# Gathering expert rows of U and V together, 8 KB each, into five joint buffers

## What is computed

```python
def block(xt):                                   # 128 tokens at a time
    qry = (xt @ w_query).reshape(128, 8, 2, 128)
    s1 = einsum('thd,kd->thk', qry[:, :, 0], keys1)
    s2 = einsum('thd,kd->thk', qry[:, :, 1], keys2)
    # top 16 of each, top 16 of their 256 sums: idx, gate
    act = gelu(einsum('td,thkd->thk', xt, expert_u[idx]))
    return einsum('thk,thkd->td', gate * act, expert_v[idx])
```

## Time and profile before

| | |
|---|---|
| median of 3 runs | 4101.56 us (4099.58 to 4101.72) |
| the profiled execution | 4101.73 us, of which the span is 4099.8 us |
| TensorE matmul busy | 3766.2 us, 92% |
| VectorE busy | 2532.3 us, 62% |
| GpSimd busy | 1789.6 us, 44% |
| ScalarE busy | 739.8 us, 18% |
| mean granted TensorE clock | 0.948 |
| moved by DMA | 1047.19 MB, mean 255 GB/s |
| gathers of U, V on GpSimd | 512 + 512 issues, 673.6 + 560.6 us |
| scatters on GpSimd | 256 issues, 412.6 us |
| dots, adds on VectorE | 512 x 1221 ns, 512 x 1285 ns |

### The profile page before, as it was taken

One profiled execution on the slowest core, in us unless ns is written; L12 is line 12 of the kernel. 1 busy time (PEld: TensorE's weight loads), 2 busy tenths in 40 slices (PEclk: granted clock), 3 DMA queues, 4 the chain that ended last, 5 costly groups with the idle time before them and its releaser, 6 DMA issues. The chain is left out here.

```text
span 4099.8 us, 43527 instructions
## 1 busy us (share of the span) xinstructions
PE 3766.2 (92%) x15978; PEld 2821.7 (69%) x15978; DVE 2532.3 (62%) x5462; ACT 739.8 (18%) x1381; POOL 1789.6 (44%) x1508
## 2 busy tenths in 40 slices
PE   8999999987899999995799999999878999999947
PEld 7856788876666666652688567888766666666526
DVE  4455215838767676877844452158387677668777
ACT  2243302211000000000222433022111000000002
POOL 3001103777555455555530021037774554555665
PEclk9899999998999999997897999999989999999978
DMA  3301134549999999999623011445599999999996
GB/s 106 113 31 42 58 144 144 134 117 327 409 410 403 409 400 410 406 409 400 235 84 113 31 42 59 145 142 134 124 331 409 410 408 408 402 410 399 409 403 243
DMA packets 332164, 1047.19 MB, mean 255 GB/s; under 512 B 79024, under 2 KB 96048, under 8 KB 313008
## 3 DMA queue, kind: packets, MB, share of 16 engines
q0 software_dynamic: 184320, 537.08, 35.8%
q1 hardware_dynamic: 130576, 488.45, 31.3%
q10 hardware_dynamic: 17056, 18.88, 1.3%
HBM read 1008.49 MB, written 35.78 MB: 255 GB/s over the span
## 5 line engine op out<-in xcount | busy, mean ns | idle before, releaser
L1733 PE MATMUL bank<-v_tile,shared 128*128 128x512 f32 x2048 | 906.2, 597 | 31.9 <-DVE shared L2136 30.2
L2198 POOL DMA_INDIRECT u_rows<-in_peer_u,idx_all x512 | 673.6, 1316 | 541.1 <-DVE act_u L2093 444.5
L2105 DVE SCALAR_TENSOR_TENSOR x<-v_rows,act_w,x 128x1024 f32<-128x1024 f32 x512 | 657.8, 1285 | 349.9 <-DMA v_rows<-in_peer_v,idx_all 331.9
L2093 DVE CUSTOM_DVE_ANT_0 u_rows<-u_rows,h 128x1024 f32<-128x1024 f32 x512 | 610.0, 1221 | 194.8 <-DMA u_rows<-in_peer_u,idx_all 193.1
L1733 PEld LDWEIGHTS bank<-v_tile,shared 128*128 128x128 f32 x2048 | 391.6, 192 | 485.2 <-issue 444.6
L2198 POOL DMA_INDIRECT v_rows<-in_peer_v,idx_all x512 | 560.6, 1095 | 370.7 <-DVE x L2105 275.0
L2208 POOL DMA_INDIRECT first_cells<-first_gate,cell_all x256 | 412.6, 1612 | 593.4 <-DVEq L2085 467.0
L1721 PE MATMUL bank<-hT,bT 128*128 128x256 f32 x2048 | 452.5, 379 | 0.0
L1721 PEld LDWEIGHTS bank<-hT,bT 128*128 128x128 f32 x2048 | 388.4, 190 | 72.0 <-issue 22.0
L1625 PE MATMUL bank<-hT,ring 128*128 128x256 f32 x1536 | 341.6, 383 | 14.3 <-PEq L152 14.2
L1625 PEld LDWEIGHTS bank<-hT,ring 128*128 128x128 f32 x1536 | 293.9, 192 | 56.9 <-issue 16.2
(11 more groups left out here) (406 smaller groups left out, 4547.8 us busy)
## 6 DMA issues: line engine op xcount, KB each, us to landing
v_tile<-in_peer_v SPq DMA_DIRECT2D x256, 512.0 KB, 7.4
ring<-in_w_in_panels SPq DMA_DIRECT2D x76, 1024.0 KB
bT<-in_peer_ut SPq DMA_DIRECT2D x128, 512.0 KB, 8.1
ring<-in_peer_w_query SPq DMA_DIRECT2D x32, 1024.0 KB
aT<-in_peer_ut SPq DMA_DIRECT2D x64, 512.0 KB, 7.2
sT<-in_peer_ut SPq DMA_DIRECT2D x64, 512.0 KB, 7.0
first_cells<-zeros SPq DMA_DIRECT2D x16, 1024.0 KB, 11.0
ring<-in_w_abv SPq DMA_DIRECT2D x16, 1024.0 KB
```

Source lines behind the costliest of these rows:

```text
L1733: ins = mm(acc[t][part][:, :], act_pair[p % AHEAD][:, at:at + P], v_tile[:, e % DENSE, part * 512:part * 512 + 512], start=(e == 0), stop= ...
L2093: nc.vector.tensor_tensor_reduce(out=u[:, n % RINGS, :], in0=u[:, n % RINGS, :], in1=h[:, t, :], scale=1.0, scalar=0.0, op0=ALU.mult, op1= ...
L2105: stt(out=m.x[:, 2 + t, :], in0=vr[:, n % RINGS, :], scalar=act_w[:, p % 4, i:i + 1], in1=m.x[:, 2 + t, :], op0=ALU.mult, op1=ALU.add).the ...
L2198: nc.gpsimd.indirect_dma_start(out=rows[:, n % RINGS, :], out_offset=None, in_=table, in_offset=bass.IndirectOffsetOnAxis(ap=idx_all[:, t, ...
```

## The change

U and V are laid side by side in DRAM as one table `peer_uv` of 8 KB rows. One gather brings both halves of a row into one of five joint buffers `uv_rows` (the same space as before). VectorE alternates now: `dot(n)`, then `add_row(n-2)`. The weight of each row is made on ScalarE: GELU of one column, then a copy with the gate as scale. A buffer comes free at its add only. LAG falls to 1, so that the list has one chunk step after chunk 63 and not two. GpSimd keeps the scatters of two heads (32) behind the first rows, not of one (16), as 8 in each of the first four chunks, not 4; 96 stand ahead of the first gather.

The diff, without the declarations:

```diff
+ROWS_BEHIND = 2
-LAG = 2
+LAG = 1
+LATE_HEADS = 2
-        u = sb("u_rows", [P, RINGS, D])
-        vr = sb("v_rows", [P, RINGS, D])
+        uv = sb("uv_rows", [P, RINGS, 2 * D])
             def chunk(c):                                     # ScalarE
-                if c < CHUNKS:
-                    act.wait_ge(s.u_free, STEP * (c + 1))
-                    f(act_g[:, c % 4, :], act_u[:, c % 4, :], ACT.Gelu_apprx_tanh).then_inc(s.gelu_done, 1)
+                if c == CHUNKS:
+                    return
+                for i in range(STEP):
+                    n = c * STEP + i
+                    t, col = slot(n)
+                    one = slice(i, i + 1)
+                    act.wait_ge(s.dotted, n + 1)
+                    f(act_g[:, c % 4, one], act_u[:, c % 4, one], ACT.Gelu_apprx_tanh).then_inc(s.gelu_done, 1)
+                    act.wait_ge(s.gelu_done, n + 1)
+                    f(act_w[:, c % 4, one], act_g[:, c % 4, one], ACT.Copy, scale=gate_all[:, t, col:col + 1]).then_inc(s.weighed, 1)
+            def dot(n):                                       # VectorE
+                t, _ = slot(n)
+                k = n // STEP % 4
+                v.wait_ge(m.uv_landed[n % RINGS], arrivals(n))
+                nc.vector.tensor_tensor_reduce(out=uv[:, n % RINGS, 0:D], in0=uv[:, n % RINGS, 0:D], in1=h[:, t, :], scale=1.0, scalar=0.0,
+                                               op0=ALU.mult, op1=ALU.add, accum_out=act_u[:, k, n % STEP:n % STEP + 1]).then_inc(s.dotted, 1)
+            def add_row(n):
+                t, _ = slot(n)
+                k = n // STEP % 4
+                v.wait_ge(s.weighed, n + 1)
+                if n:
+                    v.wait_ge(s.uv_free, n)
+                stt(out=m.x[:, 2 + t, :], in0=uv[:, n % RINGS, D:], scalar=act_w[:, k, n % STEP:n % STEP + 1], in1=m.x[:, 2 + t, :],
+                    op0=ALU.mult, op1=ALU.add).then_inc(s.uv_free, 1)
             def chunk(c):
+                for n in range(c * STEP, (c + 1) * STEP):
+                    if n < ROWS:
+                        dot(n)
+                    if ROWS_BEHIND <= n < ROWS + ROWS_BEHIND:
+                        add_row(n - ROWS_BEHIND)
-            def fetch(n, free, rows, table, sems):            # GpSimd
+            def fetch(n):
...
                 if n >= RINGS:
-                    pool.wait_ge(free, n - RINGS + 1)
+                    pool.wait_ge(s.uv_free, n - RINGS + 1)
                 nc.gpsimd.indirect_dma_start(
-                    out=rows[:, n % RINGS, :], out_offset=None, in_=table,
+                    out=uv[:, n % RINGS, :], out_offset=None, in_=table,
...
-            late = TOPK * (PEER_HEADS - 1)
+            late = TOPK * (PEER_HEADS - LATE_HEADS)
+            late_step = TOPK * LATE_HEADS // LATE_CHUNKS
             for n in range(late):
                 scatter(n)
             for n in range(RINGS):
-                fetch(n, s.u_free, u, tables[0], m.u_landed)
-            for n in range(RINGS):
-                fetch(n, s.v_free, vr, tables[1], m.v_landed)
-            for c in range(CHUNKS + LAG):
-                for n in range(STEP * c + RINGS, STEP * (c + 1) + RINGS):
-                    fetch(n, s.u_free, u, tables[0], m.u_landed)
-                for n in range(max(STEP * (c - LAG), 0) + RINGS, STEP * (c - LAG + 1) + RINGS):
-                    fetch(n, s.v_free, vr, tables[1], m.v_landed)
+                fetch(n)
+            for c in range(CHUNKS):
+                begin = STEP * (c + 1) - ROWS_BEHIND - STEP + RINGS
+                for n in range(max(begin, RINGS), min(begin + STEP, ROWS)):
+                    fetch(n)
                 if c < LATE_CHUNKS:
-                    for n in range(TOPK // LATE_CHUNKS):
-                        scatter(late + c * TOPK // LATE_CHUNKS + n)
+                    for n in range(late_step):
+                        scatter(late + c * late_step + n)
+    a["peer_uv"] = np.concatenate([a["peer_u"], a["peer_v"]], axis=-1)
```

More of the change, by code:

```diff
@@ L1396 @@
 CHUNKS_BESIDE = (0, 2, 4)
-LAG = 2
+LAG = 1
+ROWS = CHUNKS * STEP
+ROWS_BEHIND = 2
 CELLS = P * KEYS * P
@@ L1605, in arrivals @@
             k = n % RINGS
-            return 16 * (layer * len(range(k, CHUNKS * STEP, RINGS)) + n // RINGS + 1)
+            return 16 * (layer * len(range(k, ROWS, RINGS)) + n // RINGS + 1)
         block = ctx.enter_context(nc.Block())
@@ L2188, in _ @@
         def _(pool):
-            def fetch(n, free, rows, table, sems):
-                if not 0 <= n < CHUNKS * STEP:
-                    return
+            def fetch(n):
                 t, col = slot(n)
@@ L2239, in decoder_trunk @@
         m.once = once = namedtuple("Semaphores", names)(*[ctx.enter_context(nc.semaphore(n)) for n in names])
-        swdge = [ctx.enter_context(nc.semaphore(f"{n}_landed{k}")) for n in "uv" for k in range(RINGS)]
+        m.uv_landed = [ctx.enter_context(nc.semaphore(f"uv_landed{k}")) for k in range(RINGS)]
         m.scattered = ctx.enter_context(nc.semaphore("cells_scattered"))
-        m.nc, m.io, m.u_landed, m.v_landed = nc, io, swdge[:RINGS], swdge[RINGS:]
+        m.nc, m.io = nc, io
         m.banks = [ctx.enter_context(nc.psum_tensor(f"bank{k}", [P, 512], F32)) for k in range(8)]
```

32 lines of the change are left out of this document (7 added, 25 removed).

## The result

The changed kernel takes 4185.7 us (median of 4 runs, 4179.1 to 4195.8) against 4101.6 us for the kernel before in the same comparison. The ratio is 1.0206, 95% interval [1.0181, 1.0230]: slower by 84 us. The forecast was 4135 with a range to 4180, so the side was right and the size was not. The profiled execution took 4181.6 us with a span of 4179.8.

What follows compares the result with a forecast made beforehand. It took full TensorE and DMA in mid-layer, then gathers and VectorE's last rows, as the bound. Per layer 0 (start) + 14.5 (hold) - 2 (rate) + 4 (end) = 16.5 us; two layers 33, so 4135 us, range 4086 to 4180.

Steps and rivals of the forecast that it cites:

- Start of a layer: Before mid-layer: first row 16 us sooner, 5.4 left after the hot groups, 0 taken behind the store (5 faster to 7 slower).
- Smaller lags before are made up, since there TensorE sets the pace: Stretch with TensorE full, before chunk 42: lags there were expected to vanish, so no time was counted for them.
- The adds wait for ScalarE: Stretch with TensorE full: adds held for weights at chunk 42 put GpSimd 14.5 us a layer behind (9 to 18).
- The rate of 8 KB rows: Gathers under full DMA: 8 KB rows equal to 4 KB within 0 to 4%, 2 us a layer off (0 to 5).
- cost nothing: Start of a layer: the 16 more late scatters land near 3059, ahead of the store, and add no time.
- TensorE loses 0 in mid-layer: Stretch with TensorE full: TensorE may run nearly two pairs past ScalarE's chunk; 0 lost, upper end 15 us.
- rival C: Slower: 8 KB packets crowd SyncE's loads or ScalarE evicts late, TensorE gets gaps; 4165, or 4180 and over; chance 0.16.
- D: Rival: gathers are cut to 4 KB pieces, so the rate gains nothing; 4139 us; shares chance 0.50 with the forecast.
- A: Rival, faster: transfers decide and ScalarE never holds the adds; 4048 us; chance 0.22 with the 4086 case below it.
- B: Rival, no change: hold 9, start -5, rate -2 and last rows -2 a layer cancel; 4102 us; chance 0.12.
- The last rows: End of a layer, from 3980: three joint rows go round at 2.93 us a row; 92 us against 86, 6 slower.
- Behind the last landing: After the last gathered row lands: a dot, three adds and tile 2's products and sums end 1.8 us faster.

Runs made afterwards that it cites:

- e3: Changed kernel, adds two rows behind, with the gate alone as weight so no add waits for ScalarE: 4138.1 us, 1.0080 of the kernel before.
- e7: Changed kernel with each add right behind its own dot and the gate alone as weight, no wait for ScalarE: 4079.7 us, 0.9951 of the kernel before.
- g5: Changed kernel with adds one row behind and the gate alone as weight, no wait for ScalarE: 4083.8 us, 0.9956 of the kernel before.
- e11: Changed kernel, two rows behind, with ScalarE's query and score evictions moved behind the following chunk's weights: 4168.5 us, 1.0168 of the kernel before.
- e4: Changed kernel with each joint row brought by two 4 KB-row gathers, from U and V, into the same buffer: 4222.2 us, 1.0293 of the kernel before.
- e2: Kernel before with two heads of scatters behind the first rows instead of one, nothing else changed: 4113.3 us, 1.0029 of the kernel before.
- g2: e10 with its late scatters dealt out, two behind each gather, instead of in blocks: 4115.1 us, 1.0030 of the kernel before.
- e10: Changed kernel with adds one row behind and ScalarE's query and score evictions behind the following chunk's weights: 4118.0 us, 1.0043 of the kernel before.

## Why the prediction was right and wrong

**Start of a layer: right up to the hot groups, and wrong behind them.** The first dot was done at 2988.0, which is 2952.0 once the 36.0 us of layer one are taken off, 16.5 us earlier than before (forecast 16). The last hot group ended at 3065.8, 3 us earlier by the same count (forecast 5.4), and the last store is 1.4 later. The fear that a store of 1.1 KB packets is stretched by 8 KB packets did not come true: the eight stores of the two layers land in 23.0 us at most, against 26.4 before. The estimate of 38 us that the forecast drew from the Trainium skill (DMA: Bandwidth & Descriptors, "Queues, rings and completion order") is not borne out here. But the account ended at the store, and TensorE's first `values` come 7.5 us later in layer one (9.7 in layer two, by the same count), because there, between 985 and 1060, TensorE waits 27.0 us for ScalarE, where it had waited 16.6 us for a load.

**"Smaller lags before are made up, since there TensorE sets the pace": the step that failed.** I ended the account of the start at the store and took 0. From the end of the hot groups to row 40 the changed kernel loses 26.3 us in layer one (136.5 against 110.2), 16 us of it as transfer time missing by 1260. The hot groups ended 5.3 us earlier, so row 40 is 21 us late, row 60 34, row 150 28. It was not made up, for two reasons. The DMA is as full as TensorE in the earlier trace rows, at a share of 1.03, so there is little to win back with: 408 GB/s against 405 from 1260 to 1600, 2.5 us. And the adds' waits for ScalarE empty the queue again and again. Without these waits (e3) the forecast's sentence comes close to true: 17 us late at row 40, 6 at row 150. What made the lag up to row 40 is in the main the held buffers: it is 17 us with two rows held and no tie, and turns into a lead of 8 to 11 us in e7 and g5.

**"The adds wait for ScalarE", 14.5 us a layer at chunk 42: the mechanism is real, its place and size were wrong.** The missing transfer time of 1600 to 1850 is 4.2 + 11.7 = 15.9 us, near my number, but that is luck: e11, which takes such holds away, still has 382 GB/s from 1700 to 1850, and e3 374 with no tie at all. In these two the dots wait for rows behind VectorE's choices, as shown above. The rate alone doesn't prove the cause, since e7 and g5, with more rows in flight, move 365 and 370 there and wait for gates instead. Against that, ScalarE costs in places I had not counted: 48 us in all between e3 and the change, with 17 at queries and scores (e11). The adds waited 141.0 us in two layers, less than the 100 us a layer that I had named as the mark of being right.

**The rate of 8 KB rows: right in the rate, 2 us a layer, and too small in the whole.** A full stretch runs at 417 GB/s at a share of 1.02, against 410 at 1.03:

```profile
3450.00:3480.00 30.00, 30.00 (x103) 19.38 (x102) 19.64 (x33) 4.45 (x16) 6.56 (x7) 1.00 1.02 417
```

But I counted GpSimd's 256 saved issues as nothing; e4 puts rate and issues together at 36 us where rows in flight are few.

**Late scatters "cost nothing": wrong, 12 us in the kernel before** (e2). I had compared the last scatter with the store; what waits are the gathers behind each block, then VectorE's dots, ScalarE's GELU and the evictions behind it, and TensorE.

**TensorE loses 0 in mid-layer: right.** It is busy 640 of 640 us from 1060 to 1700. So rival C is out for mid-layer. Its thought that ScalarE, tied to VectorE, evicts late and TensorE gets gaps came true ahead of it, in the 27.0 us above, and behind it TensorE loses 8 us from 1700 to 1850 (141.08 us busy against 149.24). D is out by the packet count, A and B by the time.

**The last rows, +6 of 90 us: about right.** A joint row lands in 5.3 to 8.7 us, median 7.1, from 4050 to 4150, not 6.0. In the last 90 us before the last adds (4055 to 4145) the DMA moves 290 GB/s, against 325 in the 90 us of the earlier trace rows; 90 x 35 / 409 = 8 us. VectorE is at 72.65 of 90 there, less full than 83.80, as said. From row 200 to the last add the changed kernel still takes less time than the kernel before (210.1 against 221.5 us), because its adds no longer stand two chunks behind: the last one ends 3.9 us after the last dot, and before it was 19.2.

**Behind the last landing, -1.8: wrong sign, +5.7 (layer one +4.4).** The last add ends at 4148.3, and 31.5 us follow to the end of the span; before it was 25.8. After, ScalarE and the last adds:

```profile
4144.26 4.06 DVE L2109 SCALAR_TENSOR_TENSOR x<-uv_rows,act_w,x 128x1024 f32<-128x1024 f32 x3
4146.22 0.66 ACT L1971 ACTIVATE scores<-bank 128x256 f32<-128x256 f32 x2
4150.41 0.38 ACT L1971 ACTIVATE scores<-bank 128x256 f32<-128x256 f32 x1 [3.54 <-PE bank L1775]
4154.73 0.38 ACT L1971 ACTIVATE scores<-bank 128x256 f32<-128x256 f32 x1 [3.93 <-PE bank L1775]
4155.01 1.05 ACT L1955 ACTIVATE h<-x 128x1024 f32<-128x1024 f32 x1
```

Before (the last four adds, the last eviction, the square that opens the final embedding):

```profile
4068.52 5.45 DVE L2105 SCALAR_TENSOR_TENSOR x<-v_rows,act_w,x 128x1024 f32<-128x1024 f32 x4
4074.71 0.38 ACT L1962 ACTIVATE scores<-bank 128x256 f32<-128x256 f32 x1 [10.69 <-PE bank L1773]
4074.99 1.05 ACT L1946 ACTIVATE h<-x 128x1024 f32<-128x1024 f32 x1
```

Before, ScalarE was through with its last GELU at 4053.6 and evicted the embedding's products beside the last adds, so the square followed them by 1.0 us. Now the four weights of chunk 63 hold those evictions until 4146.22, and the square comes 6.7 us behind the last add. I had followed VectorE to the end and not ScalarE.

**The sum.** Forecast 0 + 14.5 - 2 + 4 = 16.5 us a layer. Measured, layer one: 25 us of transfer missing by 1850, 2.4 won back by 1960 (400 GB/s there against 391), 9 left over for the last rows, 4.4 behind them, 36.0 in all; layer two 44. The 9 are a remainder and not measured by themselves. Two slips in the working change nothing: with 16 scatters fewer GpSimd is free by 2933, not 2931, and 3% of rival A's 656 us are 20 us, not 17. What stays open: why every joint version in the table loses 7 to 21 us between rows 150 and 200, and how the 26 us before row 40 divide among scatters, choices and hot groups, since moving either of the first two only moved the dip; and a sixth joint buffer wasn't tried.

None of the full versions beats the kernel before. The nearest are g2 (1.0030) and e10 (1.0043): one row behind, two late heads, ScalarE's query and score evictions behind the weights.

## What to carry to other kernels

Count what a buffer is held for, not only its bytes: joining two transfers into one buffer made the first half wait for the second half's consumer, cut what was in flight from ten half rows to six, and turned each absence of the consumer into an empty queue. Where DMA and an engine are both full, a lag is made up only by the little that the DMA has left (9 us in 640 in e3), and each new wait takes that away; sum the missing transfer time stretch by stretch, from the first transfer on. Follow a wait through every engine that works in order: a gather behind scatters held VectorE's dot, the dot held ScalarE, and ScalarE's late evictions held TensorE. And when a value moves to an engine that works in order, list every wait in that engine's order and set each against the rows of slack that are left; the one that shows up in the old profile as the longest lag need not be the one that costs.

## What the runs showed of the hardware

A 1 MB gather of 8 KB rows beat two 0.5 MB gathers of 4 KB into the same buffer by 36 us (e4), and by rate alone only 417 against 409 GB/s. With ten 0.5 MB gathers in flight the size did not matter; with three rows it did. The Trainium skill (DMA: Bandwidth & Descriptors, "Rules for kernel authors") asks for 1 MiB a DMA; the runs agree in so far as few are in flight. SyncE's 0.5 MB loads took longer beside 8 KB packets (`v_tile` 10.9 us to landing, 7.4 before) and this cost nothing that can be seen up to 1700, since TensorE kept 640 of 640 us. And the time of a kernel of this kind varies more than its first three runs let me think: the kernel before gave 4084 to 4122 us in its later runs, where I had taken 0.2% for what can be told apart.
